# Normed halves 64 bytes later, and three equal products for each weight tile

## The chip, the core and the metric

The kernel runs as one program on one core of a Trainium2 chip. The metric is device time in microseconds (us), from the start of a launch to its end, as the median of several runs. Of its engines four matter: TensorE (PE, with its weight loads as PEld), VectorE (DVE), ScalarE (ACT), and SyncE (SP), whose queue issues the transfers.

## The reference, cut to what matters

A 256-token sequence of width 1024 goes through two blocks of two layers. In both blocks a layer is a gated network, a mixing stage and a second gated network, each behind a normalization; `reference()` runs one block on the other's output.

```python
def swiglu_ffn(h, w_gu, w_down):                  # first block
    gate, up = jnp.split(h @ w_gu, 2, axis=-1)
    return (jax.nn.silu(gate) * up) @ w_down

def swiglu(h, w_gate, w_up, w_down):              # second block
    return (jax.nn.silu(h @ w_gate) * (h @ w_up)) @ w_down

merged = sigmoid(gate_a) * (y_a @ w_proj_a) + sigmoid(gate_b) * (y_b @ w_proj_b)
x = x + merged @ w_out                            # mixing output, first block
```

So there are eight networks (1024 to 2 x 2816 and back). The mixing stages are, in the first block, a recurrence with a spatial gate, twice; in the second, a forgetting attention and an attention with three dilations.

## The kernel before

All products are made of fp32 numbers split in two: a number's rounded part "hi" (dtype fp32r) and the rest "lo". A product of weights w and activations a is taken as w_hi·a_hi + w_hi·a_lo + w_lo·a_hi, three products of 256 tokens for each 128x128 weight tile, 768 columns in all.

Weights are streamed from memory in units of 16 tiles (1 MB) through three slots of `raw_units`. ACT writes a unit's hi half tiles into `split_halves` (L933), DVE subtracts to get lo (L1347), eight tiles ("a half") at a time through four slots. DVE does three halves ahead of PE (`keep_ahead`), PE waits on `lo_ready`, and gives slots back with `halves_used` and `lin_filled`. A plan made when the program is built fixes the order of units, banks and transfers.

PE multiplies in two ways. `three` (L2036 to L2039) takes the three products as three instructions of 256 columns, all added into one 256-column half of a PSUM bank. It serves most mixing products: `two_tiles` calls it with the normed halves `h_split`, with the spatial and recurrent outputs (`ya_hi`, `ya_lo`, `yb_hi`, `yb_lo`) and the attention outputs (`o_split`); `first_tiles` calls it with `rough_split`, the early start of a stage. L2083 to L2085 (`tokens_major`) and L2602 to L2604 are the same three products with the roles turned: the normed halves are the weights, the split halves move.

`pair_tiles` (L2148, L2149) and the down product in `ffn` (L2211, L2212) take two instructions. In `h_split` and in `hidden_split` the hi and lo of a 128-row chunk lie side by side (1 KB each). So w_hi multiplies both in one instruction of 512 columns, whose result fills both halves of a bank, and w_lo multiplies hi in one of 256 columns, added into the first half. The two halves of the bank are added afterwards (ACT L1044, DVE L1473). `pair_tiles` serves gate and up of the networks, and the two mixing outputs of the first block. Counting instructions, it treats 2688 tiles (320 in each of eight networks, 64 in each of two mixing outputs), the down product 1408 (176 a network).

`place` (in `build_program`) lays tensors one behind another in each partition of the on-chip memory, in the order of the calls. Counted in bytes a partition, `split_halves` takes 32768, `x` 8192, `h_split` 16384. `h_split` therefore begins 40960 bytes behind the start of `split_halves`, 320 times 128. The area for the stages ("arena", with `hidden_split`, the ya, yb and `o_split`) begins 81344 bytes behind it, 635.5 times 128. All tiles, chunks and slots inside these tensors are multiples of 512 bytes. So against a weight tile `h_split` stands at 0 modulo 128 bytes, and those of the arena at 64. (`rough_split` has rows of 258 and stands at changing offsets.)

Of the kernel before, what the change touches and what calls it, by code (L numbers as in the profile page):

```python
# [403 lines left out]
def build_program(nc, src, out):  # L404
# [16 lines left out]

    raw = place("raw_units", [P, RAW_SLOTS, TPU * P])
    split = place("split_halves", [P, SPLIT_SLOTS, 2, HALF * P], F32R)
    x = place("x", [P, DT, T])
    h = place("h_split", [P, DT, 2, T], F32R)[:].rearrange("p c a t -> p a c t")
    pieces_at = at[0]
# [2 lines left out]
    const = place("constants", [P, NCONST])  # L429
    level_masks = place("level_masks", [P, len(LEVELS), 2, SUB], I8)  # L430
    cols = place("columns", [P, NCOLS])
    mod = place("modulation", [P, 144])
    c_rows = place("condition_rows", [P, D])
    gain2 = place("modulated_gain", [P, 6, DT])
    gate2 = place("residual_gate", [P, 6, DT])
# [302 lines left out]
    def pairs(bank):  # L738
        return bank.rearrange("p (a t) -> p a t", a=2)
# [90 lines left out]
    with nc.Block() as block:  # L830
# [1190 lines left out]
        def _(pe):  # L2021
# [13 lines left out]
            def three(o, w_hi, w_lo, a_hi, a_lo, start, stop, skip=False):  # L2035
# [2 lines left out]
                M(o, w_hi, a_lo, start=False, stop=False, skip_group_check=skip)  # L2038
                return M(o, w_lo, a_hi, start=False, stop=stop, skip_group_check=skip)  # L2039

            def two_tiles(w, key, acts, ready=None):

                bank = bank_for(key)
                if ready is not None:

                    halves = [half_ready(w), half_ready(w + 1)]
                    for k in range(DT):
                        ready(k)
                        for i in range(2):
                            s = halves[i]  # L2050
                            hi, lo = acts[i]
                            t = slice(k * P, (k + 1) * P)
                            ins = three(bank[:, i * T:(i + 1) * T], s[:, 0, t], s[:, 1, t], hi[:, k, :], lo[:, k, :],
                                        k == 0 and i == 0, k == DT - 1 and i == 1, skip=True)
                            if k == DT - 1:
                                ins.then_inc(halves_used if i == 0 else lin_filled, 1)
                    return
                for i in range(2):
                    s = half_ready(w + i)
                    hi, lo = acts[i]  # L2060
                    for k in range(DT):
                        t = slice(k * P, (k + 1) * P)
                        ins = three(bank[:, i * T:(i + 1) * T], s[:, 0, t], s[:, 1, t], hi[:, k, :], lo[:, k, :],
                                    k == 0, k == DT - 1)
                    if i == 0:
                        ins.then_inc(halves_used, 1)
                ins.then_inc(lin_filled, 1)
# [69 lines left out]
            def pair_tiles(w, banks, ready=None):  # L2137
# [4 lines left out]
                for e, k in order:  # L2142
                    if ready and e == 0:
                        ready(k)
                    if not ready and k == 0:
                        halves.append(half_ready(w + e))
                    s, t = halves[e], slice(k * P, (k + 1) * P)
                    M(pairs(banks[:, e, :]), s[:, 0, t], h[:, :, k, :], start=k == 0, stop=False)  # L2148
                    ins = M(banks[:, e, 0:T], s[:, 1, t], h[:, 0, k, :], start=False, stop=k == DT - 1)  # L2149
                    if k == DT - 1:  # L2150
                        ins.then_inc(halves_used if e == 0 else lin_filled, 1)

# [31 lines left out]
            def ffn(i):  # L2184
# [10 lines left out]
                for d in range(4):  # L2195
# [4 lines left out]
                    for e in range(2):  # L2200
                        bank = down_banks(d)[:, e, :]
                        for k in range(FT):
# [5 lines left out]
                                pe.wait_ge(hidden_ready, FT * i + k + 1)  # L2208
                            s = split[:, w % SPLIT_SLOTS, :, :]
                            t = slice(flat % HALF * P, (flat % HALF + 1) * P)  # L2210
                            M(pairs(bank), s[:, 0, t], hidden[:, :, k, :], start=k == 0, stop=False)  # L2211
                            ins = M(bank[:, 0:T], s[:, 1, t], hidden[:, 0, k, :], start=False, stop=k == FT - 1)  # L2212
                            last = e == 1 and k == FT - 1
                            if last:
                                ins.then_inc(lin_filled, 1)
# [608 lines left out]
```

## Time and profile before

| | |
|---|---|
| time, median of 3 runs | 2850.39 us (2848.18 to 2853.56) |
| profiled execution, span | 2841.6 us |
| what lies around the span | 8.8 us, as the median less the span |
| PE busy, PEld busy | 2764.1 us (97%), 2462.2 us (87%) |
| DVE busy, ACT busy | 2132.9 us (75%), 1571.2 us (55%) |
| chain that ended last | PE 83%, DVE 10%, ACT 4% |
| mean granted TensorE clock | 0.994 |

The trace gives the profiled execution by its span alone, so the profiled execution's own time is taken as span plus 8.8 us. An instruction of PE is shown with a start and a modelled end; matmuls overlap, so their durations add up to more than the time they take. What one costs in a stream is the distance from its start to the next start. Over a stretch that is (last start - first start) / (count - 1) of one line's instructions, which gives the time of a whole tile, since each tile has one instruction of each line. The modelled duration moves with that distance and tells steady streams apart at a glance.

### The profile page before, as it was taken

The page shows a single profiled execution, that of the slowest core. Times are in us where ns is not written, and L with a number is a line of the kernel's source. Part 1 is how long each engine was busy: PE and PEld are TensorE (multiplying, and loading weights), DVE is VectorE, ACT ScalarE, POOL GpSimd, SP SyncE. Part 2 cuts the span into 40 slices and gives each one's busy share as a digit, 9 for nine tenths or more (in the row PEclk, how much of TensorE's full clock was granted, in tenths as well). Part 3 has the DMA queues.
Part 4 walks back from the last instruction along what each step waited for, and adds up shares of the span by engine and source line. Part 5 has one row for each costly group of instructions (what it writes and reads, how often), then busy time and mean ns, then how long its engine had stood idle before and what let it go on. Part 6 is the DMA issues. An engine that isn't in the chain of part 4 may idle for free.

```text
span 2841.6 us, 52962 instructions
## 1 busy us (share of the span) xinstructions
PE 2764.1 (97%) x22276; PEld 2462.2 (87%) x22276; DVE 2132.9 (75%) x3179; ACT 1571.2 (55%) x2377; POOL 14.4 (1%) x23
## 2 busy tenths in 40 slices
PE   7999999999999999999999999999999999998999
PEld 7889888888888898788888888888888879998888
DVE  7877667688788787666788797667878876777764
ACT  6645644456555455544465565566546546666653
POOL 0000000000000000000000000000000000000000
PEclk9999999999999999999999999899999999999999
DMA  6774311246756743111557566433675764332454
GB/s 232 255 289 179 123 47 47 91 164 230 265 214 255 292 174 128 61 47 46 193 208 264 201 252 259 170 119 134 243 265 210 259 231 164 146 137 104 162 186 141
DMA packets 72910, 510.60 MB, mean 180 GB/s; under 512 B 8481, under 2 KB 9249, under 8 KB 11873
## 3 DMA queue, kind: packets, MB, share of 16 engines
q1 hardware_dynamic: 72672, 507.22, 48.8%
q8 instruction: 176, 2.88, 0.4%
q14 instruction: 62, 0.50, 0.0%
HBM read 506.13 MB, written 1.05 MB: 178 GB/s over the span
## 4 chain that ended last, share of the span: by engine, by line
PE 83%; DVE 10%; ACT 4%; issue 2%; DMA 1%; SPq 0%; DVEq 0%; ACTq 0%
PE solve_banks L2148 14%; PE solve_banks L2211 11%; PE solve_banks L2149 7%; PE linear_banks L2148 7%; PE solve_banks L2212 5%; PE linear_banks L2037 4%; PE linear_banks L2149 4%; PE linear_banks L2038 4%; PE linear_banks L2039 4%; PE linear_banks L2602 3%; DVE split_halves L1347 3%; PE linear_banks L2603 3%; PE linear_banks L2604 3%; PE solve_banks L2464 1%; PE linear_banks L2430 1%
## 5 line engine op out<-in xcount | busy, mean ns | idle before, releaser
L1347 DVE TENSOR_TENSOR split_halves<-raw_units,split_halves 128x1024 fp32r<-128x1024 f32 x806 | 972.1, 1222 | 314.2 <-ACT split_halves L933 311.8
L933 ACT ACTIVATE split_halves<-raw_units 128x1024 fp32r<-128x1024 f32 x806 | 841.6, 1054 | 436.7 <-PE solve_banks L2212 189.5
L2148 PE MATMUL solve_banks<-h_split,split_halves 128*128 128x512 f32 x1792 | 628.2, 394 | 3.3 <-DVE split_halves L1347 3.1
L2149 PE MATMUL solve_banks<-h_split,split_halves 128*128 128x256 f32 x1792 | 501.0, 280 | 0.0
L2211 PE MATMUL solve_banks<-hidden_split,split_halves 128*128 128x512 f32 x1408 | 498.2, 398 | 0.0
L2148 PEld LDWEIGHTS solve_banks<-h_split,split_halves 128*128 128x128 f32 x1792 | 335.8, 187 | 82.3 <-DVE split_halves L1347 2.4
L2212 PE MATMUL solve_banks<-hidden_split,split_halves 128*128 128x256 f32 x1408 | 395.6, 281 | 0.0
L2149 PEld LDWEIGHTS solve_banks<-h_split,split_halves 128*128 128x128 f32 x1792 | 338.1, 189 | 0.0
L2211 PEld LDWEIGHTS solve_banks<-hidden_split,split_halves 128*128 128x128 f32 x1408 | 264.7, 188 | 65.2
L2148 PE MATMUL linear_banks<-h_split,split_halves 128*128 128x512 f32 x896 | 314.9, 394 | 4.5 <-DVE split_halves L1347 4.5
L2212 PEld LDWEIGHTS solve_banks<-hidden_split,split_halves 128*128 128x128 f32 x1408 | 264.3, 188 | 0.1
L2149 PE MATMUL linear_banks<-h_split,split_halves 128*128 128x256 f32 x896 | 250.4, 279 | 0.0
L2602 PE MATMUL linear_banks<-split_halves,h_split 128*128 128x256 f32 (+1 forms) x784 | 229.7, 293 | 9.0 <-DVE h_split L1426 8.9
L2037 PE MATMUL linear_banks<-h_split,split_halves 128*128 128x256 f32 x736 | 225.6, 307 | 3.0 <-DVE split_halves L1347 1.9
L2603 PE MATMUL linear_banks<-split_halves,h_split 128*128 128x256 f32 (+1 forms) x784 | 224.5, 286 | 0.0
L2604 PE MATMUL linear_banks<-split_halves,h_split 128*128 128x256 f32 (+1 forms) x784 | 224.4, 286 | 0.0
L2038 PE MATMUL linear_banks<-h_split,split_halves 128*128 128x256 f32 x736 | 208.5, 283 | 0.0
L2039 PE MATMUL linear_banks<-h_split,split_halves 128*128 128x256 f32 x736 | 208.1, 283 | 0.0
L2148 PEld LDWEIGHTS linear_banks<-h_split,split_halves 128*128 128x128 f32 x896 | 167.9, 187 | 43.7 <-issue 4.1
L1451 DVE CUSTOM_DVE_ANT_0 raw_units<-raw_units,condition_rows,modulation 128x1024 f32<-128x1024 f32 x144 | 184.7, 1283 | 3.0
L2149 PEld LDWEIGHTS linear_banks<-h_split,split_halves 128*128 128x128 f32 x896 | 169.0, 189 | 0.0
L2602 PEld LDWEIGHTS linear_banks<-split_halves,h_split 128*128 128x128 f32 x784 | 154.0, 196 | 14.5 <-issue 11.3
(335 smaller groups left out, 4818.8 us busy)
## 6 DMA issues: line engine op xcount, KB each, us to landing
raw_units<-in_stream SPq DMA_DIRECT2D x403, 1024.0 KB, 4.8
raw_units<-in_mod_w SPq DMA_DIRECT2D x72, 1024.0 KB, 6.0
x<-in_x SPq DMA_DIRECT2D x4, 256.0 KB, 4.3
w2a<-in_w2a SPq DMA_DIRECT2D x2, 512.0 KB, 6.2
w_rows<-in_w SPq DMA_DIRECT2D x2, 512.0 KB, 8.0
bs_rows<-in_bs SPq DMA_DIRECT2D x2, 512.0 KB, 8.8
spatial_t<-in_ws_t SPq DMA_DIRECT2D x2, 512.0 KB, 10.0
out<-x SPq DMA_DIRECT2D x4, 256.0 KB, 4.3
```

The costliest lines, as they stand in the source:

```text
L933: nc.scalar.activation(split[:, n % SPLIT_SLOTS, 0, :], raw[:, item % RAW_SLOTS, (n % 2) * HALF * P:(n % 2 + 1) * HALF * P], ACT.Copy).the ...
L1347: V.tensor_tensor(split[:, n % SPLIT_SLOTS, 1, :], raw[:, item % RAW_SLOTS, (n % 2) * HALF * P:(n % 2 + 1) * HALF * P], split[:, n % SPLIT ...
L2037: M(o, w_hi, a_hi, start=start, stop=False, skip_group_check=skip)
L2038: M(o, w_hi, a_lo, start=False, stop=False, skip_group_check=skip)
L2039: return M(o, w_lo, a_hi, start=False, stop=stop, skip_group_check=skip)
L2148: M(pairs(banks[:, e, :]), s[:, 0, t], h[:, :, k, :], start=k == 0, stop=False)
L2149: ins = M(banks[:, e, 0:T], s[:, 1, t], h[:, 0, k, :], start=False, stop=k == DT - 1)
L2211: M(pairs(bank), s[:, 0, t], hidden[:, :, k, :], start=k == 0, stop=False)
L2212: ins = M(bank[:, 0:T], s[:, 1, t], hidden[:, 0, k, :], start=False, stop=k == FT - 1)
L2602: M(o, a_hi, s[:, 0, m], start=(c == 0 and j == 0), stop=False, skip_group_check=True)
L2603: M(o, a_lo, s[:, 0, m], start=False, stop=False, skip_group_check=True)
L2604: ins = M(o, a_hi, s[:, 1, m], start=False, stop=(c == DT - 1 and j == NCH - 1), skip_group_check=True)
```

## The change

Two edits. The tensor `modulation` (144 numbers, 576 bytes a partition) is placed ahead of `x` and `h_split`, not behind `columns`. `x`, `h_split`, `squares`, `v_first`, `constants`, `level_masks` and `columns` begin 576 bytes (four times 128, and 64) later; everything from `condition_rows` on, the arena among it, stays where it was. And a new function `three_apart` takes the place of the two instructions in `pair_tiles` and in the down product: three instructions of 256 columns, w_hi·a_hi into the first half of the bank, w_hi·a_lo into the second, w_lo·a_hi into the first.

```diff
     split = place("split_halves", [P, SPLIT_SLOTS, 2, HALF * P], F32R)
+    mod = place("modulation", [P, 144])
     x = place("x", [P, DT, T])
     h = place("h_split", [P, DT, 2, T], F32R)[:].rearrange("p c a t -> p a c t")
...
     cols = place("columns", [P, NCOLS])
-    mod = place("modulation", [P, 144])
     c_rows = place("condition_rows", [P, D])
...
+            def three_apart(bank, w_hi, w_lo, a, start, stop):
+
+                M(bank[:, 0:T], w_hi, a[:, 0, :], start=start, stop=False, skip_group_check=True)
+                M(bank[:, T:2 * T], w_hi, a[:, 1, :], start=False, stop=stop, skip_group_check=True)
+                return M(bank[:, 0:T], w_lo, a[:, 0, :], start=False, stop=stop, skip_group_check=True)
...
-                    M(pairs(banks[:, e, :]), s[:, 0, t], h[:, :, k, :], start=k == 0, stop=False)
-                    ins = M(banks[:, e, 0:T], s[:, 1, t], h[:, 0, k, :], start=False, stop=k == DT - 1)
+                    ins = three_apart(banks[:, e, :], s[:, 0, t], s[:, 1, t], h[:, :, k, :], k == 0, k == DT - 1)
...
-                            M(pairs(bank), s[:, 0, t], hidden[:, :, k, :], start=k == 0, stop=False)
-                            ins = M(bank[:, 0:T], s[:, 1, t], hidden[:, 0, k, :], start=False, stop=k == FT - 1)
+                            ins = three_apart(bank, s[:, 0, t], s[:, 1, t], hidden[:, :, k, :], k == 0, k == FT - 1)
```

The program for PE grows from 17,475 matmuls to 21,571, each with its weight load: 4096 more of each. The programs of DVE, ACT and SP keep every row and its place. On PE, where the first network goes from its early tiles (`rough_split`) to the first tiles with the normed halves (`h_split`), before:

```order
L2037 MATMUL solve_banks<-rough_split,split_halves 128x256
L2038 MATMUL solve_banks<-rough_split,split_halves 128x256
L2039 MATMUL solve_banks<-rough_split,split_halves 128x256
L2148 MATMUL solve_banks<-h_split,split_halves 128x512
L2149 MATMUL solve_banks<-h_split,split_halves 128x256
```

The same place now (L2043 to L2045 are the lines of `three_apart`):

```order
L2037 MATMUL solve_banks<-rough_split,split_halves 128x256
L2038 MATMUL solve_banks<-rough_split,split_halves 128x256
L2039 MATMUL solve_banks<-rough_split,split_halves 128x256
L2043 MATMUL solve_banks<-h_split,split_halves 128x256
L2044 MATMUL solve_banks<-h_split,split_halves 128x256
L2045 MATMUL solve_banks<-h_split,split_halves 128x256
```

The 512-column row has become two of 256 with the same weights; the early tiles are as they were. On PE, where the first network's down product ends and the next stage's norm sums (`squares`) and early tiles begin, before:

```order
L2211 MATMUL solve_banks<-hidden_split,split_halves 128x512
L2212 MATMUL solve_banks<-hidden_split,split_halves 128x256
L2167 MATMUL solve_banks<-squares,constants 128x256 x2
L2037 MATMUL linear_banks<-rough_split,split_halves 128x256
L2038 MATMUL linear_banks<-rough_split,split_halves 128x256
L2039 MATMUL linear_banks<-rough_split,split_halves 128x256
```

And now (the norm sums stand on L2172, since the file has grown):

```order
L2043 MATMUL solve_banks<-hidden_split,split_halves 128x256
L2044 MATMUL solve_banks<-hidden_split,split_halves 128x256
L2045 MATMUL solve_banks<-hidden_split,split_halves 128x256
L2172 MATMUL solve_banks<-squares,constants 128x256 x2
L2037 MATMUL linear_banks<-rough_split,split_halves 128x256
L2038 MATMUL linear_banks<-rough_split,split_halves 128x256
L2039 MATMUL linear_banks<-rough_split,split_halves 128x256
```

Here too one row is two, and nothing around it has moved.

## Rows read from the trace of the kernel before

**Rows 1.** The page: span; busy time of the engines.

```profile
span 2841.6 us, 52962 instructions
...
PE 2764.1 (97%) x22276; PEld 2462.2 (87%) x22276; DVE 2132.9 (75%) x3179; ACT 1571.2 (55%) x2377; POOL 14.4 (1%) x23
```

**Rows 2.** Stretches: busy PE, PEld, DVE, ACT, POOL; then clock, DMA share, GB/s.

```profile
31.00:204.00 173.00, 172.98 (x992) 150.80 (x992) 139.90 (x188) 97.57 (x139) 1.67 (x1) 1.00 0.71 262
...
2330.00:2663.00 333.00, 313.39 (x2708) 300.25 (x2706) 238.99 (x327) 218.23 (x327) 0.00 (x0) 0.98 0.36 133
```

**Rows 3.** One line's instructions: L2148, third network; duration min/median/max, first, last start.

```profile
L2148 PE MATMUL solve_banks<-h_split,split_halves x208: 391/391/467, 823.6 to 928.7; 128*128 128x512 f32 x104
L2148 PE MATMUL linear_banks<-h_split,split_halves x111: 391/391/391, 829.2 to 933.9; 128*128 128x512 f32 x111
```

**Rows 4.** L2148 in the second network and a mixing output, same view.

```profile
L2148 PE MATMUL solve_banks<-h_split,split_halves x206: 395/398/403, 640.4 to 746.8; 128*128 128x512 f32 x103
L2148 PE MATMUL linear_banks<-h_split,split_halves x112: 395/398/467, 634.7 to 741.8; 128*128 128x512 f32 x112
...
L2148 PE MATMUL solve_banks<-h_split,split_halves x56: 393/398/499, 600.3 to 619.8; 128*128 128x512 f32 x56
```

**Rows 5.** L2211 in the last network's down product, same view.

```profile
L2211 PE MATMUL solve_banks<-hidden_split,split_halves x176: 389/397/398, 2774.5 to 2836.3; 128*128 128x512 f32 x176
```

**Rows 6.** Three 256-column products with the normed halves: L2037, L2602, L2083, same view.

```profile
L2037 PE MATMUL linear_banks<-h_split,split_halves x150: 280/283/283, 228.2 to 281.9; 128*128 128x256 f32 x150
...
L2602 PE MATMUL linear_banks<-split_halves,h_split x59: 281/283/283, 2346.0 to 2366.8; 128*128 128x256 f32 x59
...
L2083 PE MATMUL linear_banks<-split_halves,h_split x32: 283/283/387, 299.7 to 311.0; 128*128 128x256 f32 x32
```

**Rows 7.** L2037 on the attention outputs, both attention stages, same view.

```profile
L2037 PE MATMUL linear_banks<-o_split,split_halves x30: 276/276/276, 2637.0 to 2646.9; 128*128 128x256 f32 x30
...
L2037 PE MATMUL linear_banks<-o_split,split_halves x30: 281/281/281, 1942.7 to 1953.0; 128*128 128x256 f32 x30
```

**Rows 8.** L2037 on the projections' halves, three stretches, same view.

```profile
L2037 PE MATMUL linear_banks<-yb_hi,split_halves x29: 276/276/276, 1383.7 to 1393.2; 128*128 128x256 f32 x29
...
L2037 PE MATMUL linear_banks<-ya_hi,split_halves x13: 281/281/281, 566.8 to 571.0; 128*128 128x256 f32 x13
L2037 PE MATMUL linear_banks<-yb_hi,split_halves x11: 281/281/281, 571.4 to 574.9; 128*128 128x256 f32 x11
...
L2037 PE MATMUL linear_banks<-yb_hi,split_halves x17: 276/276/276, 576.8 to 582.2; 128*128 128x256 f32 x17
```

**Rows 9.** Matmuls in order of time at 575 us: start, duration, line.

```profile
575.48 0.28 PE L2039 MATMUL linear_banks<-yb_hi,split_halves 128*128 128x256 f32 x1
575.64 0.38 PE L2037 MATMUL linear_banks<-yb_hi,split_halves 128*128 128x256 f32 x1
575.86 0.28 PE L2038 MATMUL linear_banks<-yb_lo,split_halves 128*128 128x256 f32 x1
```

**Rows 10.** Matmuls in order of time where the first network begins.

```profile
31.22 0.47 PE L2148 MATMUL solve_banks<-h_split,split_halves 128*128 128x512 f32 x1
31.53 0.28 PE L2149 MATMUL solve_banks<-h_split,split_halves 128*128 128x256 f32 x1
31.64 0.40 PE L2148 MATMUL solve_banks<-h_split,split_halves 128*128 128x512 f32 x1
```

**Rows 11.** Waits: engine, line waited for, total us, times, longest.

```profile
PE linear_banks L2037 <- DVE split_halves L1347: 19.9, 9, 15.6
PE solve_banks L2561 <- DVE logits L1943: 9.2, 10, 1.8
...
ACT split_halves L933 <- PE solve_banks L2212: 189.5, 120, 3.5
```

**Rows 12.** Weight loads by line; the page's queue of instructions.

```profile
L2149 PEld LDWEIGHTS solve_banks<-h_split,split_halves 128*128 128x128 f32 x1792 | 338.1, 189 | 0.0
...
q8 instruction: 176, 2.88, 0.4%
```

## The prediction

> **What bounds the kernel now.** I read the page first. PE is busy 2764.1 of 2841.6 us [rows 1]. That share alone proves little, since ends of matmuls are modelled, so I took the stretches next. In the first network, 31 to 204 us, PE shows no gap, while DVE is busy 139.9 of 173 us, ACT 97.6, and the transfers take 0.71 of their engines' time [rows 2]. Third, the waits: what ACT waits for in the networks is mostly PE giving slots back, 189.5 us in 120 waits on one line [rows 11]. So in a network the split weights stand ready and PE alone sets the pace; whatever a weight tile costs on PE is paid in full, 4096 times in the edited places. In the mixing stages PE is still nearly alone: it is busy 313.4 of 333 us in the dilated attention [rows 2], and its largest waits for another engine are 19.9 us for split weights and 9.2 us for logits over the whole run [rows 11].
>
> So the question is what one weight tile (768 columns) costs. The view of one line's instructions gives it, as the distance between first and last start over the count less one.
>
> - 512 and 256 columns, `h_split`: 110.3 us over 318 distances, 347 ns, in the third network [rows 3]; 112.1 over 317, 353.6 ns, in the second, and about the same in a mixing output [rows 4]. Six networks run as the first kind (first, third, fourth, fifth, seventh, eighth), two as the second (second, sixth), each from its beginning to the end of its 320 tiles.
> - 512 and 256 columns, `hidden_split`: 61.8 us over 175, 353 ns [rows 5], so in all eight.
> - three of 256, with `h_split` as moving operand or as weights: 53.7 us over 149, 360 ns, and about 359 and 364 (a stop in it) on the other two lines [rows 6].
> - three of 256, with the arena's tensors moving: 9.9 us over 29 and 10.3 over 29, on the same line and the same tensor: 341 and 355 ns [rows 7]. On the projections 9.5 over 28 and 5.4 over 16, but 8.1 over 23 [rows 8]. Pooled, the short kind takes 24.8 us over 73, 340 ns; the long one 18.4 over 52, 354 ns.
>
> The modelled durations separate these without arithmetic: 276, 281, 283 ns, each with min and median alike. A stream keeps its price: it falls into one spacing at its start and stays there. It changes at a stop: at 575.64 us an instruction comes 160 ns behind the one before, and the stream, 281 until then, is 276 afterwards [rows 8, 9]. I call this a lock.
>
> What divides 360 from 340 or 354? In all three lines of [rows 6] the normed halves and the weight tiles have the same place modulo 128 bytes. In [rows 7, 8] the moving operand stands 64 bytes off the weights. The edit that moves `h_split` by 576 bytes puts the normed halves at 64 off as well, and `hidden_split` is there already.
>
> **The change part by part.**
>
> *Networks and mixing outputs.* 2688 tiles with `h_split`: 1920 now at 347 (six networks), 768 at 353.6 (two networks and the mixing outputs); 1408 with `hidden_split` at 353. In the short lock, 340: 1920 x 7 + 768 x 13.6 + 1408 x 13 ns = 13.4 + 10.4 + 18.3 = 42.1 us less. In the long lock, taken at 353.5 (354 within the rounding of the starts): 1920 x 6.5 = 12.5 us more, the rest as now. These are the two ends of this term.
>
> *Mixing products with the normed halves.* Nothing in their order changes, only the place. 1632 tiles (736 on L2037, 768 on L2602, 128 on L2083), of which 256 stand in 128 runs of two tiles between the recurrence's small products, too short to settle. The others: 1376 x 20 = 27.5 us less in the short lock, 1376 x 6.5 = 8.9 us less in the long one. On L2602 and L2083 the normed halves are the weights; I take the same prices for them, and zero as the other end.
>
> *Which lock.* The trace cannot tell it beforehand. Of the 47 streams with the arena's tensors that begin behind a stop or another product, 26 settle short and 21 long; those of [rows 7, 8] are three short, two long. A network is one such stream per lock: it starts behind a wait, the first instruction stands 0.31 us ahead of the next and the following ones are in step at once [rows 10]. Nothing interrupts it until the down product is over, and a lock passes from one tensor to the next where both stand at 64 (281 on ya, then 281 on yb, [rows 8]). So I expect about eight separate draws, and choose 5 of 8 short, a little over what was counted, as six of eight networks agree now. Networks: 5/8 x (-42.1) + 3/8 x 12.5 = -26.3 + 4.7 = -21.6 us. Mixing, with many starts, at 26/47: -(0.55 x 27.5 + 0.45 x 8.9) = -19.1, of which I take nine tenths, -17.2, as PE is busy 94% of the dilated attention [rows 2].
>
> *More instructions.* 4096 more matmuls and weight loads. A load lasts 189 ns [rows 12] but is overlapped: in [rows 6 to 8] loads already follow each other at every 113 to 120 ns with nothing missing. The bound below is nothing; above, the 13 ns a tile by which three products exceed two at the old place, which the first rival holds. Their fetching: 2.88 MB for 52,962 instructions now [rows 1, 12], so some 0.45 MB more for 8192, against transfers that have 29% free in a network. I take nothing.
>
> *Other moved tensors.* `x`, `squares`, `constants` and the rest keep 64-byte alignment on 64-byte alignment, and instructions of DVE and ACT keep their rows. A few hundred small products use `constants`; I take nothing, with 3 us as an estimate either way (some 600 at 5 ns).
>
> *What is late next.* At 340 ns a unit of 16 tiles takes 5.44 us. DVE's work in the first network, 139.9 of 173 us, then fills 83% instead of 81%. Nothing new waits.
>
> **Sum.** Span 2841.6 - 21.6 - 17.2 = 2802.8 us; with the 8.8 us around it, 2811.6, as against the median of 2850.4. I say 2811 us.
>
> **What the pages say.** The trace gave two prices for one line by where its operand stands. The Trainium skill (SBUF — State Buffer, "SBUF: two separate sides") says that PE never waits on another user of that memory, and (TensorE: Matmul & The Clock Gate, Part 2, step 1) that loading weights takes no read bandwidth from a running matmul. By that an operand's place would cost nothing; the trace disagrees, with 360 against 340 and 354 ns. The same page, "Back-to-back issue gap", has a fixed 2.5 ns on top of each matmul's columns: 4096 more would cost 10 us as an estimate. That speaks against the change; the trace has three products cheaper than the pair in the first of [rows 7] and dearer in [rows 6].
>
> **The rivals.**
>
> *All long.* Every network falls into the long lock, as ya did at 566 us. Networks +12.5, mixing at nine tenths of 8.9, -8: +4.5, 2855 us. For it: two locks of five rows. Against it: eight independent starts.
>
> *The place is not the cause.* In every 283 ns row the normed halves lie hi beside lo; in every 276 or 281 row hi and lo are far apart. If that layout decides, or the plain number of instructions does, three products cost 360 with `h_split` and `hidden_split` wherever they stand: 1920 x 13 + 768 x 6.4 + 1408 x 7 = 25.0 + 4.9 + 9.9 = +39.8, nothing gained in mixing: 2890 us. It decides from a price of over 353 ns a tile. Against it: on L2602 and L2083 the moving operand has hi and lo 4 KB apart, and the price is 360 too [rows 6]. (It is where the page's fixed cost per matmul would show, at a fifth of the size.)
>
> *All short.* Networks -42.1, mixing -27.5 x 0.9 = -24.8: 2783.5 us.
>
> **How the numbers follow.** Mixed locks (three to seven networks short), 2790 to 2835 us: 0.56. All short, some 2780 to 2790: 0.22. All long or nearly, 2843 to 2857: 0.14. Place not the cause, 2870 to 2895: 0.08. Range 2779 to 2848: it takes in the first two, and a part of the third; 2783.5 less the 3 us of `constants` makes its lower end. What can be told from no change is about 0.2%, 5.7 us. Faster by more: 0.56 + 0.22 + a quarter of the third, 0.82. Within: 0.09. Slower: 0.08 and a bit of the third, 0.09.
>
> **What would show it.** In the view of one line's instructions the three lines of `three_apart` should have a median of 276 or 281 ns, one value through a whole network, and 340 or 354 ns from tile to tile; L2037 and L2602 with the normed halves should have left 283. DVE, ACT and transfers should keep their counts and times. 283 on the new lines says that the place was not the cause. Gaps on PE within a network, ended by DVE or a transfer, would say that the slack was misjudged; a spacing not in this list, that alternating between the halves of a bank has a price of its own.

## The result, and the profile after

| | before | after |
|---|---|---|
| median | 2849.28 us (2846.9 to 2853.56, 4 runs) | 2833.91 us (2825.14 to 2837.7, 4 runs) |
| profiled execution, span | 2841.6 us | 2823.4 us |

The ratio is 0.9938, with a 95% interval of 0.9924 to 0.9951: the change makes the kernel 0.6% faster, 15 us by the medians and 18.2 us from profile to profile. The forecast was 39 us. The time lies within the range, and 15 of the 39 us came. The profiled execution of the changed kernel is the fastest of its four.

First the page of the changed kernel, beside [rows 1, 12]: span, busy time, the queue of instructions.

```profile
span 2823.4 us, 61154 instructions
...
PE 2742.8 (97%) x26372; PEld 2622.2 (93%) x26372; DVE 2130.7 (75%) x3179; ACT 1567.9 (56%) x2377; POOL 14.0 (0%) x23
...
q8 instruction: 208, 3.41, 0.5%
```

PE has 4096 more matmuls and the queue of instructions 0.53 MB more. Neither shows as time: in the stretches, which answer to [rows 2] (PE, PEld, DVE, ACT, POOL, clock, DMA share, GB/s), the first network has no gap on PE, and DVE has as much slack as it had.

```profile
31.00:205.00 174.00, 174.00 (x1479) 174.00 (x1479) 136.95 (x185) 94.89 (x138) 1.09 (x1) 1.00 0.71 260
...
2310.00:2643.00 333.00, 311.37 (x2768) 297.67 (x2767) 243.34 (x331) 221.72 (x330) 0.00 (x0) 0.99 0.38 140
```

Then the view on which everything rests, one line's instructions (duration min/median/max, first and last start), answering to [rows 3 to 5]. It shows the fifth network's gate and up, its down product, the first network's gate and up, and the last down product.

```profile
L2043 PE MATMUL solve_banks<-h_split,split_halves x208: 276/276/356, 1621.5 to 1724.6; 128*128 128x256 f32 x104
L2043 PE MATMUL linear_banks<-h_split,split_halves x112: 276/276/276, 1627.0 to 1730.1; 128*128 128x256 f32 x112
...
L2043 PE MATMUL solve_banks<-hidden_split,split_halves x175: 281/281/281, 1730.4 to 1791.9; 128*128 128x256 f32 x175
...
L2043 PE MATMUL solve_banks<-h_split,split_halves x206: 279/279/279, 31.4 to 137.8; 128*128 128x256 f32 x103
L2043 PE MATMUL linear_banks<-h_split,split_halves x112: 279/279/279, 36.4 to 143.4; 128*128 128x256 f32 x112
...
L2043 PE MATMUL solve_banks<-hidden_split,split_halves x176: 280/281/281, 2756.3 to 2818.2; 128*128 128x256 f32 x176
```

In the edited places the two spacings of the prediction are there and no others. The fifth network's gate and up take (1730.1 - 1621.5) / 319 = 340 ns a tile, 276 throughout ("short" from here on). The first one's take (143.4 - 31.4) / 317 = 353, 279 throughout ("long"). Reading the distance for every tile of the eight networks: 340.0 ns in the second, fifth, sixth and seventh, 353.3 in the first, third, fourth and eighth, each without a change inside. But the down product runs at 353.3 ns in all of its twelve streams (a stream is a stretch without a stop; stops cut the fourth network's into five), also behind the networks at 340. Here are PE's instructions in order of time, where the fifth network goes from `h_split` to `hidden_split`:

```profile
1730.06 0.28 PE L2043 MATMUL linear_banks<-h_split,split_halves 128*128 128x256 f32 x1
1730.17 0.28 PE L2044 MATMUL linear_banks<-h_split,split_halves 128*128 128x256 f32 x1
1730.29 0.28 PE L2045 MATMUL linear_banks<-h_split,split_halves 128*128 128x256 f32 x1
1730.40 0.28 PE L2043 MATMUL solve_banks<-hidden_split,split_halves 128*128 128x256 f32 x1
1730.52 0.28 PE L2044 MATMUL solve_banks<-hidden_split,split_halves 128*128 128x256 f32 x1
1730.64 0.28 PE L2045 MATMUL solve_banks<-hidden_split,split_halves 128*128 128x256 f32 x1
```

PE does not stop here. The starts are 110 to 120 ns apart, first at the 113 of the short spacing, and from 1730.40 us at 118: the short spacing is lost at the change of operand. The mixing products, answering to [rows 6], left 283 as expected: on L2037 for 279 or 276, on L2606 (L2602 before) mostly for 276.

```profile
L2037 PE MATMUL linear_banks<-h_split,split_halves x148: 279/279/385, 228.3 to 280.7; 128*128 128x256 f32 x148
...
L2037 PE MATMUL linear_banks<-h_split,split_halves x146: 276/276/276, 1022.5 to 1071.8; 128*128 128x256 f32 x146
...
L2606 PE MATMUL linear_banks<-split_halves,h_split x56: 276/276/415, 2329.9 to 2349.7; 128*128 128x256 f32 x56
```

Summing the distances from start to next start over all tiles of a kind (a distance over 400 ns, behind a stop, counted as 400) shows where the time went. The rows reach from the first matmul to the last, and add up to 17.5 of the 18.2 us:

| PE, us | before | after | forecast |
|---|---|---|---|
| gate and up, mixing outputs | 938.1 | 933.9 (-4.2) | -10.2 |
| down product | 497.6 | 497.8 (+0.2) | -11.4 |
| mixing, normed halves moving | 413.1 | 409.3 (-3.8) | |
| mixing, normed halves as weights | 346.7 | 334.4 (-12.3) | -17.2, both |
| all other products, and stops | 625.4 | 628.0 (+2.6) | 0 |

### The profile page after: what moved, and what is told of

Its sections match the earlier page's. It is cut to its first block, busy times and chain, and to the rows that moved or that the text cites. A ratio compares the mean times of both kernels' runs of the same rounds, so it can differ in the third digit from the quotient of the medians.

```text
span 2823.4 us, 61154 instructions
## 1 busy us (share of the span) xinstructions
PE 2742.8 (97%) x26372; PEld 2622.2 (93%) x26372; DVE 2130.7 (75%) x3179; ACT 1567.9 (56%) x2377; POOL 14.0 (0%) x23
## 4 chain that ended last, share of the span: by engine, by line
PE 83%; DVE 10%; ACT 4%; issue 2%; DMA 1%; SPq 0%; DVEq 0%; ACTq 0%
PE solve_banks L2043 13%; PE solve_banks L2045 13%; PE solve_banks L2044 13%; PE linear_banks L2037 4%; PE linear_banks L2043 4%; PE linear_banks L2045 4%; PE linear_banks L2044 4%; PE linear_banks L2038 4%; PE linear_banks L2039 3%; DVE split_halves L1347 3%; PE linear_banks L2606 3%; PE linear_banks L2607 3%; PE linear_banks L2608 3%; PE solve_banks L2468 1%; PE linear_banks L2434 1%
## 5 line engine op out<-in xcount | busy, mean ns | idle before, releaser
L2043 PE MATMUL solve_banks<-h_split,split_halves 128*128 128x256 f32 x1792 | 498.4, 278 | 3.3 <-DVE split_halves L1347 3.1
L2045 PE MATMUL solve_banks<-h_split,split_halves 128*128 128x256 f32 x1792 | 498.1, 278 | 0.0
L2044 PE MATMUL solve_banks<-h_split,split_halves 128*128 128x256 f32 x1792 | 497.5, 278 | 0.0
L2043 PE MATMUL solve_banks<-hidden_split,split_halves 128*128 128x256 f32 x1408 | 396.0, 281 | 0.0
L2045 PE MATMUL solve_banks<-hidden_split,split_halves 128*128 128x256 f32 x1408 | 395.7, 281 | 0.0
L2044 PE MATMUL solve_banks<-hidden_split,split_halves 128*128 128x256 f32 x1408 | 395.7, 281 | 0.0
L2043 PEld LDWEIGHTS solve_banks<-h_split,split_halves 128*128 128x128 f32 x1792 | 335.9, 187 | 4.8 <-DVE split_halves L1347 2.4
L2045 PEld LDWEIGHTS solve_banks<-h_split,split_halves 128*128 128x128 f32 x1792 | 336.4, 188 | 0.0
L2044 PEld LDWEIGHTS solve_banks<-h_split,split_halves 128*128 128x128 f32 x1792 | 336.4, 188 | 0.0
L2043 PEld LDWEIGHTS solve_banks<-hidden_split,split_halves 128*128 128x128 f32 x1408 | 267.3, 190 | 0.1
L2045 PEld LDWEIGHTS solve_banks<-hidden_split,split_halves 128*128 128x128 f32 x1408 | 267.3, 190 | 0.0
L2044 PEld LDWEIGHTS solve_banks<-hidden_split,split_halves 128*128 128x128 f32 x1408 | 264.3, 188 | 0.1
L2043 PE MATMUL linear_banks<-h_split,split_halves 128*128 128x256 f32 x896 | 249.1, 278 | 4.9 <-DVE split_halves L1347 4.9
L2045 PE MATMUL linear_banks<-h_split,split_halves 128*128 128x256 f32 x896 | 249.0, 278 | 0.0
L2044 PE MATMUL linear_banks<-h_split,split_halves 128*128 128x256 f32 x896 | 248.6, 278 | 0.0
L2606 PE MATMUL linear_banks<-split_halves,h_split 128*128 128x256 f32 (+1 forms) x784 | 225.7, 288 | 9.3 <-DVE h_split L1426 8.9
L2037 PE MATMUL linear_banks<-h_split,split_halves 128*128 128x256 f32 x736 | 223.9, 304 | 3.8 <-DVE split_halves L1347 2.6
L2607 PE MATMUL linear_banks<-split_halves,h_split 128*128 128x256 f32 (+1 forms) x784 | 220.2, 281 | 0.0
L2608 PE MATMUL linear_banks<-split_halves,h_split 128*128 128x256 f32 (+1 forms) x784 | 220.1, 281 | 0.0
L2038 PE MATMUL linear_banks<-h_split,split_halves 128*128 128x256 f32 x736 | 206.5, 281 | 0.0
```

The source lines that it names most:

```text
L2037: M(o, w_hi, a_hi, start=start, stop=False, skip_group_check=skip)
L2043: M(bank[:, 0:T], w_hi, a[:, 0, :], start=start, stop=False, skip_group_check=True)
L2044: M(bank[:, T:2 * T], w_hi, a[:, 1, :], start=False, stop=stop, skip_group_check=True)
L2045: return M(bank[:, 0:T], w_lo, a[:, 0, :], start=False, stop=stop, skip_group_check=True)
L2606: M(o, a_hi, s[:, 0, m], start=(c == 0 and j == 0), stop=False, skip_group_check=True)
L2607: M(o, a_lo, s[:, 0, m], start=False, stop=False, skip_group_check=True)
```

## The experiments

All times are medians beside runs of the kernel before on the same chip. "Ahead" and "behind" say where an operand begins against the weights, modulo 256 bytes: The distance of `hidden_split` from the weights is 64 short of a multiple of 256, so it stands 64 ahead; `h_split` stood at 0, and moved by 576 it stands 64 behind. What an experiment says of single networks is read from its one profiled run.

**1. The place alone.** The move of `modulation` without `three_apart`.

```diff
+    mod = place("modulation", [P, 144])
     x = place("x", [P, DT, T])
```

> The 576-byte move alone; networks, mixing outputs and down product keep their two instructions of 512 and 256 columns. Theory: the mixing products with the normed halves leave the one spacing of 360 ns a tile for 340 or 354, which in the changed kernel's profile was worth about 14 us; the pair on the moved halves runs like the pair on the down product's operand, which also stands 64 bytes off: 353 ns in all networks instead of 347 in six, 1920 x 6.7 = 13 us more. Sum about 1 us less, 2848 us. Rival (the place is not the cause of the mixing gain): mixing stays at 360 and the pair at 347 and 353, 2849 us, no line changes. The times are close; the traces part them.

Measured 2844.05 us against 2852.17, ratio 0.9973 (0.9964 to 0.9983). A network of it and a line of the dilated attention:

```profile
L2148 PE MATMUL solve_banks<-h_split,split_halves x206: 392/397/398, 826.8 to 933.2; 128*128 128x512 f32 x103
L2148 PE MATMUL linear_banks<-h_split,split_halves x109: 392/397/398, 831.8 to 937.8; 128*128 128x512 f32 x109
...
L2602 PE MATMUL linear_banks<-split_halves,h_split x58: 276/276/387, 2354.8 to 2374.9; 128*128 128x256 f32 x58
```

Both halves of the theory hold. The mixing line has left 283 for 276. Its moving operand, the split halves, was not moved, only the normed halves that are its weights: what counts is the place of one operand against the other. On the networks the pair of 512 and 256 takes (937.8 - 826.8) / 314, 353 ns, in all eight, so its cheaper spacing of 347 is gone. By the distances the networks are 12.6 us dearer and the mixing products 15.0 us cheaper than in the profile of before. The rival falls. By the medians the time was 8 us lower, not 1. The two profiles do not show that: this one is the second slowest of ten runs, and its span of 2846.8 us is 5.2 longer than that of before; all other products and stops take 6.9 us more in it. See below on the profile that the sum began from.

**2. Three products alone.** `three_apart` without the move.

```diff
-    mod = place("modulation", [P, 144])
     x = place("x", [P, DT, T])
...
+    mod = place("modulation", [P, 144])
     c_rows = place("condition_rows", [P, D])
```

> Three products a tile in networks, mixing outputs and down product, with the normed halves where they were before. Theory (the place decides): all streams with the normed halves show 360 ns a tile; 1920 x 13.3 + 768 x 6.7 = 30.7 us more; the down product, 64 bytes off as ever, stays at 353 or falls to 340 in some networks. 2880 us, less up to 19 us if the down product were short. Rival (three products are as cheap at the old place, and the gain of the change came with the number of instructions): 340 or 353 in the networks, 2835 to 2850 us.

Measured 2860.33 us, ratio 1.0031 (1.0018 to 1.0044): slower. The third network's gate and up, and its down product:

```profile
L2043 PE MATMUL solve_banks<-h_split,split_halves x206: 282/283/283, 828.9 to 937.2; 128*128 128x256 f32 x103
L2043 PE MATMUL linear_banks<-h_split,split_halves x112: 283/283/283, 833.9 to 943.0; 128*128 128x256 f32 x112
...
L2043 PE MATMUL solve_banks<-hidden_split,split_halves x174: 276/276/276, 944.1 to 1002.9; 128*128 128x256 f32 x174
```

With the normed halves at 0 every network is at 283, 360 ns a tile. So the place decides, and the second rival of the prediction falls. Not foreseen: the down product is at 276, 340 ns, behind all eight networks. It takes 480.0 us in all, 17.6 less than before. A stream at 0 hands the short spacing on to one 64 ahead; a stream 64 behind, as in the changed kernel, hands it the long one, whether it was short or long itself.

**3. The down product's operand 128 bytes later**, so that both stand 64 behind.

```diff
-    hidden = over("hidden_split", [P, FT, 2, T], 0, F32R)
+    hidden = over("hidden_split", [P, FT, 2, T], 0.125, F32R)
```

> The changed kernel, with the down product's operand 128 bytes later, so that it stands at the same place modulo 256 bytes as the moved normed halves (both 64 behind the weights; in the changed kernel it stands 64 ahead). Theory A (a spacing is handed on from gate and up to the down product only where both operands have the same place modulo 256): each down product then runs at the spacing of its own network, 340 or 353, with four of eight short 704 x 13.3 = 9.4 us less, about 2824 us. Theory B (the down product itself cannot take the short spacing, by its longer chains, its wait or its banks): 353.3 ns in all twelve of its streams again, about 2834 us.

Measured 2824.35 us, ratio 0.9906 (0.9878 to 0.9935). The second network (gate and up, down) and the third:

```profile
L2043 PE MATMUL linear_banks<-h_split,split_halves x110: 276/276/276, 637.5 to 739.9; 128*128 128x256 f32 x110
...
L2043 PE MATMUL solve_banks<-hidden_split,split_halves x176: 276/276/276, 745.6 to 805.1; 128*128 128x256 f32 x176
...
L2043 PE MATMUL linear_banks<-h_split,split_halves x111: 280/280/280, 824.7 to 931.4; 128*128 128x256 f32 x111
...
L2043 PE MATMUL solve_banks<-hidden_split,split_halves x172: 280/280/280, 932.5 to 992.9; 128*128 128x256 f32 x172
```

Each down product has the spacing of its own network: 276 behind 276, 280 behind 280, in eight of eight (two networks short). Theory A holds, theory B falls.

**4. The normed halves 192 bytes later**, so that both stand 64 ahead: `modulated_gain` (192 bytes) is placed ahead of `x`, and `modulation` stays at its old place.

```diff
-    mod = place("modulation", [P, 144])
+    gain2 = place("modulated_gain", [P, 6, DT])
     x = place("x", [P, DT, T])
```

> The changed kernel, with the normed halves 192 bytes later than before instead of 576 (another tensor is placed ahead of them), so that they stand 64 bytes ahead of the weights modulo 256, just as the down product's operand does. Theory A (handed on where the place modulo 256 is the same): each down product runs at its network's spacing; with half of the networks short about 9 us less than the changed kernel, 2824 us, and more or less with the number of short networks. Theory B (the down product itself): 353.3 ns in all of its streams, about 2834 us. A third theory, that 64 ahead and 64 behind have different prices, shows in the networks as a spacing that is not 340 or 353.

Measured 2822.51 us, ratio 0.9897 (0.9876 to 0.9918). The third network (gate and up, down), and L2606:

```profile
L2043 PE MATMUL linear_banks<-h_split,split_halves x111: 276/276/276, 827.6 to 930.3; 128*128 128x256 f32 x111
...
L2043 PE MATMUL solve_banks<-hidden_split,split_halves x173: 276/276/276, 931.3 to 989.8; 128*128 128x256 f32 x173
...
L2606 PE MATMUL linear_banks<-split_halves,h_split x55: 279/279/363, 2344.9 to 2364.8; 128*128 128x256 f32 x55
```

Again each down product has the spacing of its network, eight of eight, four of them short (at the seventh a stop of 0.33 us stands between the two, so there it may be a new draw). Modulo 512 bytes the two operands stand 256 apart here, and still the spacing is handed on. But the side has an effect on how a stream settles behind a stop. On L2606, where the normed halves are the weights, the moving operand now stands behind, and one stream of 51 is short; in the changed kernel it stands ahead, and 42 of 51 are (streams of six tiles or more). On L2037 it is the other way round, 9 of 14 short with the moving operand ahead against 2 of 14 behind.

**5 to 8. Choosing the spacing.** If a stream at 0 has one spacing and hands on the short one, a few products at 0 behind the wait should set a whole network. Weights against weights stand at 0. Into the kernel of experiment 4 go n products behind the wait with which each network and each mixing output begins. They write a bank that the next product starts anew, and nothing of them is kept.

```diff
                         ready(k)
+                        if k == 0:
+                            for _ in range(6):
+                                M(banks[:, 0, 0:T], halves[0][:, 0, 0:P], halves[0][:, 0, 0:T], start=True, stop=True,
+                                  skip_group_check=True)
```

Six products:

> The kernel with the normed halves 192 bytes later (normed halves and down operand both 64 bytes ahead of the weights, modulo 256), and behind the wait at the start of each network and mixing output six extra products of 256 columns, in which weights move against weights (0 modulo 256), written into a bank that the next product starts anew. Theory (a stream at 0 is always in its one spacing of 120 ns, and hands on the short spacing to one 64 ahead, as it did to eight of eight down products with three products at the old place): all eight networks run at 340 ns from gate and up through the down product; against four of eight, 4 x 496 x 13.3 = 26 us less, the 60 extra products 7 us more: about 2803 us. Rival (chance at each start): three to five of eight short, 2829 us.

Measured 2815.62 us, ratio 0.9878 (0.9861 to 0.9895). In the profile seven of eight networks are short, gate and up and down; the fifth is long. That is short of the expected eight and of 2803 us, but more than the four of experiment 4.

The same six in the kernel of experiment 3 (both operands behind):

> The kernel with the down operand 128 bytes later (normed halves and down operand both 64 bytes behind the weights, modulo 256), with the same six extra products at the starts. Whatever a stream at 0 hands on to one 64 behind, it should be the same in all eight networks: all short, about 2800 us, or all long, about 2845 us. Since streams 64 behind settled long in twelve of fourteen runs of the mixing stages, long is likelier. Rival (chance at each start): a mixture, some 2831 us.

Measured 2841.66 us, ratio 0.997 (0.9959 to 0.9981). Six of eight networks long, the last two short: mostly the long one, as thought likelier, but not one answer for all eight. Either way each down product has its network's spacing.

Three products, as in experiment 5:

```diff
-                            for _ in range(6):
+                            for _ in range(3):
```

> As with six extra products 64 ahead, but three of them. If the one spacing at 0 is reached within three products, all eight networks are short, about 2800 us (3.6 us cheaper than with six). If it takes more, the networks are mixed, near 2825 us.

Measured 2804.72 us (2803.15 to 2807.91), ratio 0.9841 (0.9825 to 0.9857). In order of time, the start of the third network (the early tiles, the three extra products as one row, the first tile), and then its lines:

```profile
813.95 0.28 PE L2039 MATMUL solve_banks<-rough_split,split_halves 128*128 128x256 f32 x1
814.50 0.59 PE L2153 MATMUL solve_banks<-split_halves 128*128 128x256 f32 x3 [0.27 <-issue]
814.93 0.28 PE L2043 MATMUL solve_banks<-h_split,split_halves 128*128 128x256 f32 x1
815.05 0.28 PE L2044 MATMUL solve_banks<-h_split,split_halves 128*128 128x256 f32 x1
815.17 0.28 PE L2045 MATMUL solve_banks<-h_split,split_halves 128*128 128x256 f32 x1
```

```profile
L2043 PE MATMUL solve_banks<-h_split,split_halves x207: 276/276/276, 815.3 to 918.0; 128*128 128x256 f32 x104
L2043 PE MATMUL linear_banks<-h_split,split_halves x111: 276/276/277, 820.4 to 923.1; 128*128 128x256 f32 x111
...
L2043 PE MATMUL solve_banks<-hidden_split,split_halves x174: 276/276/276, 924.1 to 982.9; 128*128 128x256 f32 x174
```

All eight networks start short, and all eight down products start short. In one, the second, a stop threw gate and up into the long spacing for their last 40 tiles; its down product is short all the same, behind a small stop in its first tile:

```profile
740.84 0.28 PE L2045 MATMUL solve_banks<-h_split,split_halves 128*128 128x256 f32 x1
740.96 0.36 PE L2043 MATMUL solve_banks<-hidden_split,split_halves 128*128 128x256 f32 x1
741.15 0.28 PE L2044 MATMUL solve_banks<-hidden_split,split_halves 128*128 128x256 f32 x1
```

The last two starts are 190 ns apart and not 118. Three products cost 0.43 us at each of ten places.

The control is six products whose moving operand begins 64 bytes further, so 64 behind and not at 0.

```diff
-                                M(banks[:, 0, 0:T], halves[0][:, 0, 0:P], halves[0][:, 0, 0:T], start=True, stop=True,
+                                M(banks[:, 0, 0:T], halves[0][:, 0, 0:P], halves[0][:, 0, 16:16 + T], start=True, stop=True,
```

> The control for the six extra products: the same number at the same places, but their moving operand begins 64 bytes further, so that they stand 64 bytes off the weights, not at 0. Theory (it is the spacing at 0 that selects): networks stay mixed or go long, 2825 to 2850 us. Rival (any six products behind the wait do it, because the first ones are started out of step): all eight short as with six at 0, about 2803 us.

Measured 2852.5 us (ten runs, 2851.32 to 2854.54), ratio 1.0006 (0.9996 to 1.0015).

```profile
L2043 PE MATMUL solve_banks<-h_split,split_halves x206: 281/281/281, 825.0 to 931.4; 128*128 128x256 f32 x103
L2043 PE MATMUL linear_banks<-h_split,split_halves x111: 281/281/281, 830.0 to 936.7; 128*128 128x256 f32 x111
...
L2043 PE MATMUL solve_banks<-hidden_split,split_halves x171: 281/281/281, 937.8 to 997.8; 128*128 128x256 f32 x171
```

All eight networks are long. It is not the extra products but their place that selects. Experiments 5 and 8 are the same kernel but for the place of one operand of six extra products in front of each stream, and are 37 us apart. The control is not a neutral one: in the changed kernel too, streams 64 behind handed the long spacing to those 64 ahead. Without extra products (experiment 4) the time lies between the two, 2822.51 us.

**9. The attentions' normed halves behind.** The kernel of experiment 7, with the normed halves of the two attentions in a second tensor 128 bytes further on.

```diff
-        o = h[:, part, c, :]
+        o = (h_attention if n in (8, 11) else h)[:, part, c, :]
...
-                    a_hi, a_lo = (h[:, a, c, j * CH:(j + 1) * CH] for a in range(2))
+                    a_hi, a_lo = (h_attention[:, a, c, j * CH:(j + 1) * CH] for a in range(2))
```

> The kernel with three extra products at 0, and the normed halves of the two attentions written 128 bytes further on (64 behind the weights modulo 256, so that there, where the normed halves are the weights, the moving operand stands 64 ahead of them). Theory: streams whose moving operand stands 64 ahead settle short more often (42 of 51 runs on that line so in the changed kernel, none of 51 with the halves 192 bytes later); 768 tiles, some eight tenths of them 13.3 ns cheaper: 8 us less than with the three extra products alone, about 2797 us. Rival: the share of short runs has nothing to do with the side, 2804 us.

Measured 2805.3 us (2799.75 to 2812.18), ratio 0.9856 (0.9831 to 0.988). The line in the dilated attention:

```profile
L2612 PE MATMUL linear_banks<-split_halves,h_split x52: 276/276/386, 2345.0 to 2364.7; 128*128 128x256 f32 x52
```

On that line 37 of 51 streams are short, against none of 51 in experiment 7, and all products with the normed halves as weights take 334.5 us instead of 341.6. So the side matters. The median did not move: in this profile the last network fell long (6.6 us), which eats the gain.

**10. 128 bytes off.** The changed kernel with `one_less_ka` (64 bytes) placed ahead of `x` as well.

```diff
     mod = place("modulation", [P, 144])
+    one_less_ka = place("one_less_ka", [P, 2, DT])
     x = place("x", [P, DT, T])
```

> The changed kernel with the normed halves 640 bytes later than before, 128 bytes off the weights modulo 256. If what counts is the place modulo 128, the networks run at 360 ns a tile as at 0, and all down products then short, 340: about 2855 us. If modulo 256, a spacing of its own shows in the networks, between 340 and 360.

One run took 2848.95 us. The third network and its down product:

```profile
L2043 PE MATMUL solve_banks<-h_split,split_halves x206: 279/281/286, 826.5 to 933.7; 128*128 128x256 f32 x103
L2043 PE MATMUL linear_banks<-h_split,split_halves x111: 278/281/286, 831.5 to 939.0; 128*128 128x256 f32 x111
...
L2043 PE MATMUL solve_banks<-hidden_split,split_halves x174: 276/276/277, 940.4 to 999.3; 128*128 128x256 f32 x174
```

A spacing of its own, (939.0 - 826.5) / 316, 356 ns in all eight networks, neither 360 nor 353. So the place counts modulo 256, or more, and not modulo 128. The down products behind it are mixed, six short and two long.

**11. One extra product** in place of three, in the kernel of experiment 7.

```diff
-                            for _ in range(3):
+                            for _ in range(1):
```

> As with three extra products at 0, but one alone behind each wait. If one product at 0 suffices to hand on the short spacing, all eight networks are short, about 2802 us. If the spacing at 0 has to be reached first, networks are mixed as without it, 2815 to 2825 us.

Measured 2804.1 us (2794.42 to 2816.82), ratio 0.9839 (0.9807 to 0.9871). In the profile, of the slowest run, the fifth and the sixth network are long and one more down product, which has a stop in its first tile. The median is that of three products, but the four runs spread over 22 us instead of 5.

## Why the prediction was wrong

*Held.* PE alone sets the pace; the extra loads, the fetching and the other moved tensors cost nothing that shows (all other products and stops differ by 2.6 us); there are two spacings, 340 and 353 ns, one for a whole stream; leaving 0 pays in the mixing products (16.1 us, forecast 17.2). That this sum fits so well is in part luck: at its one share of 26 in 47 it holds 6.0 us for the normed halves moving and 11.2 for them as weights, and 3.8 and 12.3 came, since the two lines settle differently (2 of 14 streams short, 42 of 51).

*The step that failed.* The prediction has "a lock passes from one tensor to the next where both stand at 64". It was read from ya to yb, both in the arena and so on the same side of the weights. `h_split` was moved 576 bytes, to the other side. Both stand 64 off modulo 128, as the prediction counted, but 128 apart modulo 256. Experiments 3 and 4 each put both on one side, by moving either operand, and in sixteen of sixteen networks the down product has the network's spacing. Over experiments 3 to 9 and 11, all with both operands on one side, it is so in all 58 networks without a stop at the change; in the other six, with a stop, it changed twice. In the changed kernel none of the four short ones handed its spacing on. So the down product's term, 5/8 x 18.3 = 11.4 us, was nothing (0.2 us more were measured). From span to span 38.8 us were forecast and 18.2 came; this term is over half of the difference.

*The draw.* Five of eight short networks were forecast, four came in the profile. No trace shows the draws of the other three runs, which were 8 to 13 us slower. The count behind it, 26 of 47, was taken from operands ahead of the weights and applied to one behind. On the mixing lines the two sides differ widely, as said. The networks of experiments 3 and 4, two and four short, are too few to separate the sides. With four short, gate and up gave 4.2 us and not 10.2; the four long ones had all had the cheap pair of 347 ns, and lost 6.5 ns a tile.

*The profile that the sum began from.* What lies around the span is 1.7 us in the changed kernel's profiled execution (2825.14 less 2823.4), not 8.8. With as much around its span of 2841.6, the profiled execution of before took some 2843 us, at the low end of all its timed runs (2842.41 to 2858.28). Six of its eight networks had the cheap pair; each that has not costs 320 x 6.7 = 2.1 us. So the profile was a good draw, not the median (that the draws made the difference is argued, as the other runs left no trace), and 7 us of what was added around the span weren't there: with 1.7 the sum would have read 2804.5 us, further off still. Against the median of before, the loss of the cheap pair costs less than against this profile. That fits with the median of experiment 1, 8 us faster where 1 was forecast, but was not shown by a second profile of before.

*The rivals.* "The place is not the cause" fell with experiments 1 and 2: three products at the old place cost 360 ns and lose. "All long" was true of the down product alone. Experiment 8 shows all networks long: 2852.5 us, with extra products. "All short" comes nearest in experiment 7, at 2804.72 us.

*The pages.* The same three instructions cost 360 ns a tile in experiment 2, 353 in experiment 8 and 340 in experiment 7. The Trainium skill (SBUF — State Buffer, "SBUF: two separate sides") says that PE never waits on another user of that memory. No run here shows such a wait; what the runs show is a price for the places of PE's own two operands against each other, of which that sentence says nothing. The Trainium skill (TensorE: Matmul & The Clock Gate, "Back-to-back issue gap") also gives 2.5 ns on top of a matmul's columns, for an isolated one; by it 4096 more would cost 10 us, as an estimate. The runs show three products 7 ns a tile under the cheaper pair, or 6 over it, so by their spacing and not by their number.

*What stays open.* What decides short or long behind a stop. The first starts differ by a few ns only, and profiles of the same line come out either way. Nor is it shown which unit makes one stream wait for the other. Why six products at 0 left one network long and three left none is open as well, and may be chance.

The versions of experiments 7 and 11 beat both kernels, at 0.984 of the time before.

## What to carry to other kernels

On a PE-bound kernel look at the distance from start to start, stream by stream, before pricing an instruction: here the same three products cost 340, 353, 356 or 360 ns a tile, by where the moving operand begins against the weights modulo 256 bytes and by how the stream began. In a kernel like this one, keep operands that follow one another at the same place modulo 256, off the weights' own, and start a long stream so that it falls into the cheap spacing. When a price comes from a draw, look at where the profiled run lies among the timed runs before taking that profile as the base of a sum.

## What the runs showed that was not expected

- A spacing is handed on across a change of operand: from long streams at 0 to 64 ahead short (eight of eight, experiment 2), from 64 behind to 64 ahead long (eight of eight, the changed kernel), between equal places unchanged (58 of 58 without a stop). Not every change has one answer: a few products at 0 left none to two of eight networks 64 ahead long (experiments 5, 7, 9 and 11), and behind streams 128 off two of eight were long.
- One to three extra products at 0, of 0.1 to 0.4 us, mostly decide the speed of the next 170 us of PE's work: 2804 us, against 2822.51 without them and 2852.5 with six 64 off.
- Much of the spread between runs of one kernel seems to be these draws, though each has one trace only. Where that shows all networks long, ten runs lie within 3.2 us (experiment 8); where it shows them mixed, four lie within 12.6 (the changed kernel). But in experiment 1, with all networks alike, ten lie within 7.3.
